# A one-core decoder trunk: first tiles summed earlier, the odd mixer's order changed, and 24 unread products in each round of the local attention

## The chip, the core and the metric

The kernel runs on one core of one Trainium2 chip. The metric is device time in microseconds (us) of one launch, from which a median of several runs is taken. TensorE's granted clock, shown in the profile as a share of full speed, has two levels, 1.2 and 2.4 GHz (0.50 and 1.00).

## What is computed

A two-layer decoder trunk is run over 544 tokens of width 1024: a prompt of 512 tokens and 8 sample streams of 4 tokens each, with the same weights. Each layer is: half a gated feed-forward, a mixer, an attention to 256 memory rows, and half a gated feed-forward again. The first (even) layer mixes with gated linear attention and retention; the second (odd) layer mixes with a diagonal state space (S5) beside a sliding-window attention. Cut to what matters here:

```python
def run_trunk(x, ...):
    for layer in range(2):
        x = x + 0.5 * swiglu(rms_norm(x, w['ffn1_norm'][layer]), gate, up, down)
        h = rms_norm(x, w['mix_norm'][layer])
        x = x + (gla_retention_mixer if layer % 2 == 0 else s5_swa_mixer)(h, ...)
        x = x + memory_attend(rms_norm(x, w['mem_x_norm'][layer]), ...)
        x = x + 0.5 * swiglu(rms_norm(x, w['ffn2_norm'][layer]), gate, up, down)

def s5_swa_mixer(h, ...):
    u, q, k, v = split_cols(h @ odd_w_in)
    c_out = s5_scan(u, ...)          # y = C h + D u; z = gelu(y); z * sigmoid(z @ w_glu + b)
    q, k = partial_rotary(rms_norm(q), pos), partial_rotary(rms_norm(k), pos)
    d_out = sliding_window_sink_attention(q, k, v, ...)   # window 128, 8 heads, 2 key heads
    return concatenate([c_out, d_out]) @ odd_w_out
```

## The kernel before, in words

Tokens lie along the free dimension, features on the 128 partitions; a matrix product turns 128 rows of weights and 272 tokens at a time. Every fp32 weight and activation is split in a high and a low part, and each product is three passes: high by high, high by low, low by high.

**Dense layers.** `projection` (line 105) does all of them but the mixers' and the memory's. It makes output tiles in pairs, s = 0 and 1; a tile of the feed-forward's first half has 8 steps k of 6 products (3 passes, 2 halves of the tokens), 48 in all. SP loads the weights of tile s into `raw[s]`, ACT makes the high part (line 87), DVE the low part (line 91), and TensorE runs the products (line 404). DVE then takes the tile out of PSUM: `finish_tile`, which multiplies by the RMS factor `rstd` (line 295) and, in a feed-forward, joins gate and up tile, or adds to x (line 311). With `norm` the projection also finds `rstd` itself: squares are summed by a product with ones (`sums`, line 396), then ACT takes Ln and Exp (lines 258, 261). With `prepared` the sum of squares of x and 7 of 8 source tiles are already there from the section before, so that only the last step k waits for anything. In the kernel before, the sum stands in the middle of the second tile. The projections that are both `norm` and `prepared` are three: the first halves of ffn2 in layer 0, ffn1 in layer 1 and ffn2 in layer 1. The feed-forward ffn1 of layer 0 has `norm` alone. ACT may overwrite the high weights of tile s only when TensorE has done that tile (`tile_done`).

**The odd mixer** (`odd_mixer`, line 2435) is one section in which each engine has its list of steps written out by hand. TensorE's steps are `dense(i, g)`, tile i of 14 and token half g (line 2658; tiles 0 to 9 are the input projection, 10 to 13 the gate of S5, with 4 steps k); `outputs(q)` for S5 (taps at line 2712, states at line 2716, then ACT's gelu at line 2917); `sums` and `swap` for the norm and rotation of keys and queries (lines 2727, 2736); and then the attention, which runs in five rounds: four blocks of 128 queries (3, 2, 1, 0) and the samples ("s"). Blocks 3 to 1 see 256 keys, block 0 has 128, the samples have 160. A round has two key heads kv = 0 and 1, and goes through these steps:

- `scores(r)` on TensorE (line 2777; for the samples lines 2769 and 2770, and ahead of all `cached_scores`, line 2754), two rounds ahead;
- `soft(r, kv)` on DVE: scale and mask (line 3165), maximum (3168), its negative (3170). It waits for the sink's column, which POOL writes (line 2635);
- `exps(r, kv)` on ACT (line 2951);
- `divide(r, kv)` on DVE (lines 3176 and 3178);
- `turn(r, kv)` on TensorE, the transposes of the probabilities (line 2795), and `turned_copy` on ACT (line 2965);
- `values(r)` on TensorE (line 2819; samples 2811 and 2813), and `out_copy` on ACT (lines 2976, 2973).

Besides, ACT takes four sigmoids of S5's gate (`gates`, line 2983), and POOL multiplies them in (line 2639), in the list of the kernel before behind round 0 on ACT and behind round 1's sinks on POOL. A section ends at a barrier of all engines; the next one, the output projection, splits the mixer's result (lines 264 and 356) and multiplies.

Of the kernel before, what the change touches and what calls it, by code (L numbers as in the profile page):

```python
# [104 lines left out]
def projection(nc, core, name, weights, pairs, kt, src, cols, finish, dst, scale=1.0, after=None, norm=None, scaled=False,  # L105
# [27 lines left out]
    with ExitStack() as ctx:  # L133
# [39 lines left out]
        with nc.Block(name) as block:  # L173
# [112 lines left out]
            def _(dve):  # L286
# [75 lines left out]
                def pair_parts(i):  # L362
                    for s in range(2):
                        split_low(s, i * 2 + (s + 2))
                        finish_tile(s, i)
                        next_part(i, s)
                times_range(dve, 0, last_pair, pre, pair_parts)
                if after is not None:
                    split_low(0, 2 * pairs, after[1])
                finish_tile(0, last_pair)  # L370
# [4 lines left out]
            def _(pe):  # L375
                def tile(s, i, first=False):
                    if not (first and s == 0):
                        pe.wait_ge(low_ready, i * 2 + s)
                    if not first:

                        if finish == "gate":
                            pe.wait_ge((gate_scaled, up_scaled)[s], i)
                        else:
                            pe.wait_ge(psum_free[s], i)
                    for k in range(kt):
                        if norm and first and s == 0 and prepared:
                            if k == kt - 1:
                                pe.wait_ge(last_ready, 1)
                        elif norm and first and s == 0:
                            pe.wait_ge(x_ready, k + 1)  # L390
                        if split and first and s == 0:
                            pe.wait_ge(part_ready, k + 1)
                        if norm and first and s == 1 and k == kt // 2:
                            pe.wait_ge(added, 1 if prepared else 7)
                            for a in range(groups):
                                ins = nc.tensor.matmul(sums[:, a, :], core.mats[:, ONES],
                                                       total[:, a * width:(a + 1) * width], start=True, stop=True)
                            ins.then_inc(summed, 1)
# [9 lines left out]
                for s in range(2):  # L408
                    tile(s, 0, True)
                def pair_tiles(i):  # L410
                    for s in range(2):
                        tile(s, i)
# [2022 lines left out]
def odd_mixer(nc, core, a, out, after_in):  # L2435
# [23 lines left out]
    rounds = [3, 2, 1, "s", 0]  # L2459
    NR = len(rounds)  # L2460

    with ExitStack() as ctx:
# [101 lines left out]
        with nc.Block("odd") as block:  # L2564
# [27 lines left out]
            def _(pool):  # L2592
# [32 lines left out]
                for r in range(NR):  # L2625
# [17 lines left out]
            def _(pe):  # L2643
# [58 lines left out]
                def outputs(q):  # L2702
# [6 lines left out]
                    for t in range(L):  # L2709
                        b, lo = 6 + t // 2, (t % 2) * NCH  # L2710
                        for s in range(t + 1):
                            nc.tensor.matmul(ps[:, b, lo:lo + NCH], taps[:, q, t - s, :], u_tiles[q][:, s:TOK:L],
                                             start=(s == 0), stop=False)
                        for ri in range(2):
                            for j4 in range(4):
# [818 lines left out]
```

## Time and profile before

| | us |
|---|---|
| median of 3 runs (lowest to highest) | 2762.49 (2759.56 to 2765.79) |
| the profiled execution | 2762.19 |
| its span, first to last instruction | 2760.4 |
| TensorE busy (matmuls) | 2562.1 |
| DVE, ACT, POOL busy | 1253.2, 928.2, 452.7 |
| mean granted TensorE clock | 0.96 |

The profiled execution lies 0.3 us below the median; 1.8 us of it lie around the span. TensorE has work for 93% of the span, so time is lost only where it waits and where its clock is at the lower level. The 40 slices of the page show which stretches those are: both mixers' ends, the two memory attentions, and starts of sections.

### The profile page before, as it was taken

To read this page: it belongs to the slowest core of one execution; us is meant where nothing else is said; L and a number is where in the kernel's file an instruction comes from. 1 tells how busy PE (TensorE), PEld (TensorE's weight loads), DVE (VectorE), ACT (ScalarE), POOL (GpSimd) and SP (SyncE) were. 2 spreads that over 40 slices of the span, in tenths; PEclk is the share of its full clock that TensorE was granted. 3 is DMA by queue.
4 is the path that set the end of the run, shared out by engine and by line. 5 is a ranking of instruction groups with operands and counts; after the bars stand their busy time and mean duration, and the time that the engine had idled before them with its cause. 6 is when DMAs were issued, how large, how long until landed. Compare 5 with 4: busy or idle time off the path is not lost. (4 is left out here: it accounts for less than half of the span.)

```text
span 2760.4 us, 48499 instructions
## 1 busy us (share of the span) xinstructions
PE 2562.1 (93%) x20495; PEld 2468.6 (89%) x20495; DVE 1253.2 (45%) x1606; ACT 928.2 (34%) x1128; POOL 452.7 (16%) x464
## 2 busy tenths in 40 slices
PE   6999999998988799999999999999888879999998
PEld 6999998997987699999999999997768859999998
DVE  4433435344555444334434345454655753442442
ACT  4421223222364344212234324231545532431221
POOL 0000012012412220000151464030114223000000
PEclk9999999998999899999999999999989989999999
DMA  3222223211255222222222222221114542222222
GB/s 108 90 92 77 88 88 101 100 49 57 98 178 202 96 77 84 89 79 91 90 82 91 89 76 86 89 68 50 48 47 153 191 145 77 84 88 78 85 95 75
DMA packets 79006, 257.39 MB, mean 93 GB/s; under 512 B 16100, under 2 KB 18740, under 8 KB 78368
## 3 DMA queue, kind: packets, MB, share of 16 engines
q1 hardware_dynamic: 66048, 212.89, 24.2%
q0 software_dynamic: 12832, 42.66, 4.6%
q8 instruction: 98, 1.61, 0.2%
q14 instruction: 28, 0.23, 0.0%
HBM read 245.41 MB, written 10.11 MB: 93 GB/s over the span
## 5 line engine op out<-in xcount | busy, mean ns | idle before, releaser
L91 DVE TENSOR_TENSOR w_low<-w_raw,w_high 128x1024 fp32r<-128x1024 f32 (+1 forms) x358 | 481.7, 1346 | 1031.9 <-ACT w_high L87 1031.6
L87 ACT ACTIVATE w_high<-w_raw 128x1024 fp32r<-128x1024 f32 (+1 forms) x358 | 397.5, 1111 | 1192.4 <-PE ps L404 941.9
L404 PE MATMUL ps<-ffn_hid,w_high 128*128 128x272 f32 x2816 | 476.5, 292 | 24.6 <-PEq L173 24.6
L404 PE MATMUL ps<-h_high,w_high 128*128 128x272 f32 x1920 | 404.1, 292 | 46.2 <-DVE h_low L338 15.6
L404 PEld LDWEIGHTS ps<-ffn_hid,w_high 128*128 128x128 f32 x2816 | 406.1, 192 | 26.1 <-issue 26.1
L404 PE MATMUL ps<-h_high,w_low 128*128 128x272 f32 x1920 | 401.4, 291 | 0.0
L404 PE MATMUL ps<-h_low,w_high 128*128 128x272 f32 x1920 | 401.0, 291 | 0.0
L404 PEld LDWEIGHTS ps<-h_high,w_high 128*128 128x128 f32 x1920 | 306.9, 191 | 49.9 <-DVE h_low L356 16.9
L404 PEld LDWEIGHTS ps<-h_low,w_high 128*128 128x128 f32 x1920 | 307.1, 192 | 0.0
L404 PEld LDWEIGHTS ps<-h_high,w_low 128*128 128x128 f32 x1920 | 304.6, 192 | 0.0
L404 PE MATMUL ps<-ffn_high,w_high 128*128 128x272 f32 x1408 | 292.5, 289 | 12.6 <-DVE ffn_up_sg L295 8.3
L404 PE MATMUL ps<-ffn_hid,w_low 128*128 128x272 f32 x1408 | 295.6, 292 | 0.0
L404 PE MATMUL ps<-ffn_low,w_high 128*128 128x272 f32 x1408 | 292.8, 289 | 0.0
L404 PE MATMUL ps<-ffn_high,w_low 128*128 128x272 f32 x1408 | 291.7, 289 | 0.0
L404 PEld LDWEIGHTS ps<-ffn_high,w_high 128*128 128x128 f32 x1408 | 222.2, 189 | 13.9 <-DVE w_low L91 8.7
L404 PEld LDWEIGHTS ps<-ffn_hid,w_low 128*128 128x128 f32 x1408 | 225.4, 192 | 0.0
L404 PEld LDWEIGHTS ps<-ffn_high,w_low 128*128 128x128 f32 x1408 | 222.3, 189 | 0.0
L404 PEld LDWEIGHTS ps<-ffn_low,w_high 128*128 128x128 f32 x1408 | 221.6, 189 | 0.0
L203 POOL TENSOR_TENSOR rstd<-x 128x544 f32<-128x544 f32 x7 | 7.6, 1090 | 897.8 <-DVE x L311 897.8
L627 PE MATMUL ps<-h_high,w_high 128*128 128x272 f32 (+1 forms) x400 | 123.8, 310 | 1.7 <-PEq L67 1.7
L627 PE MATMUL ps<-h_high,w_low 128*128 128x272 f32 (+1 forms) x400 | 119.5, 299 | 0.0
L627 PE MATMUL ps<-h_low,w_high 128*128 128x272 f32 (+1 forms) x400 | 119.3, 298 | 0.0
(497 smaller groups left out, 3619.9 us busy)
## 6 DMA issues: line engine op xcount, KB each, us to landing
w_raw<-in_ffn_w_gate SPq DMA_DIRECT2D x88, 512.0 KB, 3.6
w_raw<-in_ffn_w_up SPq DMA_DIRECT2D x88, 512.0 KB, 3.6
w_raw<-in_ffn_w_down SPq DMA_DIRECT2D x64, 704.0 KB, 4.1
mem_ring<-in_cache_mem_k POOLq DMA_DIRECT2D x64, 256.0 KB, 6.3
mem_ring<-in_cache_mem_v POOLq DMA_DIRECT2D x64, 256.0 KB, 6.3
w_raw<-in_even_w_in SPq DMA_DIRECT2D x24, 512.0 KB, 3.6
w_raw<-in_mem_w_q SPq DMA_DIRECT2D x16, 512.0 KB, 4.9
w_raw<-in_mem_w_k SPq DMA_DIRECT2D x16, 512.0 KB, 4.4
```

What stands on the lines that cost most here:

```text
L87: return nc.scalar.activation(core.high[s][:, 0:kt * P], core.raw[s][:, 0:kt * P], ACT.Copy)
L91: return nc.vector.tensor_tensor(core.low[s][:, 0:kt * P], core.raw[s][:, 0:kt * P], core.high[s][:, 0:kt * P].bitcast(F32), ALU.subtract)
L203: nc.gpsimd.tensor_tensor(rstd, x, x, ALU.mult).then_inc(squares_added, 1)
L404: last = nc.tensor.matmul(acc[s][:, a, :], w, x[:, k, a * width:(a + 1) * width], start=(k == 0 and n == 0), stop=(k == kt - 1 and n == 2))
L627: ins = nc.tensor.matmul(ps[0:m, g, 0:HALF], w[:, k * width:k * width + m], x[:, k, g * HALF:(g + 1) * HALF], start=(k == 0 and p == 0), s ...
```

## The change

In `projection`: the prepared first pair runs steps 0 to 6 of tile 0, then the sum of squares, then steps 0 to 6 of tile 1, and only then step 7 of both tiles. And DVE takes a finished tile out of PSUM before it makes the next low weights, where it was the other way round. In `odd_mixer`: the samples' round comes second; the gate's sigmoids come behind the exponentials of the round before the last, and POOL's four products behind all sinks; norm and rotation of the last query tiles come ahead of the gate's low parts on DVE; the scores of round 0 and of the cache come ahead of tile 11 on TensorE, with the softmax steps moved to match; the taps of S5's outputs are joined, two time steps in one product; and 24 products of 272 columns into an unused bank (8 ahead of each turn and 8 ahead of the values) are added in each round.

```diff
@@ projection, DVE @@
                     for s in range(2):
+                        finish_tile(s, i)
                         split_low(s, i * 2 + (s + 2))
-                        finish_tile(s, i)
                         next_part(i, s)
@@ projection, TensorE @@
+                def sum_squares():
+                    pe.wait_ge(added, 1 if prepared else 7)
...
+                def first_pair():
+                    if norm and prepared:
+
+                        products(0, range(kt - 1))
+                        sum_squares()
+                        pe.wait_ge(low_ready, 1)
+                        products(1, range(kt - 1))
+                        pe.wait_ge(last_ready, 1)
+                        for s in range(2):
+                            products(s, [kt - 1]).then_inc(tile_done, 1)
+                        return
@@ odd_mixer @@
-    rounds = [3, 2, 1, "s", 0]
+    rounds = [3, "s", 2, 1, 0]
@@ odd_mixer, POOL @@
-                    if r == 1:
-                        for t in range(4):
-                            pool.wait_ge(sig_ready, t + 1)
-                            nc.gpsimd.tensor_tensor(u_tiles[t], u_tiles[t], sig[:, t], ALU.mult).then_inc(gated, 1)
+                for t in range(4):
+                    pool.wait_ge(sig_ready, t + 1)
+                    nc.gpsimd.tensor_tensor(u_tiles[t], u_tiles[t], sig[:, t], ALU.mult).then_inc(gated, 1)
@@ odd_mixer, TensorE, outputs(q) @@
-                    for t in range(L):
-                        b, lo = 6 + t // 2, (t % 2) * NCH
-                        for s in range(t + 1):
-                            nc.tensor.matmul(ps[:, b, lo:lo + NCH], taps[:, q, t - s, :], u_tiles[q][:, s:TOK:L],
-                                             start=(s == 0), stop=False)
...
+                    u = u_tiles[q].rearrange("p (c s) -> p s c", s=L)
+                    for h in range(2):
+                        for d in range(2 * h + 2):
+                            t = max(2 * h, d)
+                            lo = (t - 2 * h) * NCH
+                            nc.tensor.matmul(ps[:, 6 + h, lo:2 * NCH], taps[:, q, d, :], u[:, t - d:2 * h + 2 - d, :],
+                                             start=(d == 0), stop=False)
...
@@ odd_mixer, TensorE @@
+                def keep_busy(r):
+
+                    if r == 0:
+                        pe.wait_ge(evicted, 2 * NT)
+                    for _ in range(8):
+                        nc.tensor.matmul(ps[:, 0, 0:HALF], core.h[0][:, 0, 0:P], core.h[0][:, 1, 0:HALF], start=True, stop=True)
...
                 turn_values()
+                swap(4)
                 dense(10, 0)
                 dense(10, 1)
-                swap(4)
+                scores(0)
+                cached_scores()
                 dense(11, 0)
                 dense(11, 1)
-                scores(0)
-                cached_scores()
...
                 for r in range(NR):
+                    keep_busy(r)
                     turn(r, 0)
+                    keep_busy(r)
                     turn(r, 1)
                     if r + 2 < NR:
                         scores(r + 2)
+                    keep_busy(r)
                     values(r)
@@ odd_mixer, ACT @@
-                    if r == 0:
+                    if r == NR - 2:
                         gates()
@@ odd_mixer, DVE @@
+                norm(4)
+                rotate(3)
                 z_low_part(0)
                 z_low_part(1)
-                norm(4)
+                rotate(4)
                 z_low_part(2)
                 z_low_part(3)
-                rotate(3)
+                pick_samples()
...
```

What it does to the instruction lists is shown at three places.

POOL, in the attention: line 2635 writes the sinks' columns, line 2639 multiplies by the gates. Before:

```order
L2635 TENSOR_SCALAR odd_region<-vectors 128x4 x4
L2639 TENSOR_TENSOR odd_mixed<-odd_mixed,s_gd 128x544 x4
L2635 TENSOR_SCALAR odd_region<-vectors 128x4 x2
L2635 TENSOR_SCALAR odd_region<-vectors 128x1 x2
L2635 TENSOR_SCALAR odd_region<-vectors 128x4 x2
```

and now (lines 2653 and 2656):

```order
L2653 TENSOR_SCALAR odd_region<-vectors 128x4 x2
L2653 TENSOR_SCALAR odd_region<-vectors 128x1 x2
L2653 TENSOR_SCALAR odd_region<-vectors 128x4 x6
L2656 TENSOR_TENSOR odd_mixed<-odd_mixed,s_gd 128x544 x4
```

The four gate products no longer stand ahead of any sink.

ACT, from the exponentials of the round before the last to the end, now: lines 2984 exponentials, 2998 copies of the turned probabilities, 3016 sigmoids, 3009 copies of results.

```order
L3009 ACTIVATE odd_mixed<-ps 128x4x128
L2998 ACTIVATE odd_region<-ps 128x1024
L2984 ACTIVATE odd_region,s_rot<-odd_region,s_rot 128x129 x4
L2998 ACTIVATE odd_region<-ps 128x1024
L2984 ACTIVATE odd_region,s_rot<-odd_region,s_rot 128x129 x4
L3016 ACT_TABLE_LOAD
L3016 ACTIVATE s_gd<-s_gd 128x544 x4
L3009 ACTIVATE odd_mixed<-ps 128x4x128
L2998 ACTIVATE odd_region<-ps 128x512 x2
L3009 ACTIVATE odd_mixed<-ps 128x4x128
```

The table load and the sigmoids stand behind the last exponentials and ahead of the copies of the last two results; the second table load of the list before, back to the exponentials, is gone.

TensorE, the first round of the attention, now: 2851 the added products, 2818 turns, 2800 scores, 2842 values.

```order
L2851 MATMUL ps<-h_high 128x272 x8
L2818 MATMUL ps<-mats,odd_region 128x128 x8
L2851 MATMUL ps<-h_high 128x272 x8
L2818 MATMUL ps<-mats,odd_region 128x128 x8
L2800 MATMUL ps<-odd_k,odd_mixed 128x256 x8
L2851 MATMUL ps<-h_high 128x272 x8
L2842 MATMUL ps<-odd_region,s_rot 64x512 x4
```

Between any two steps of a round that wait for another engine there are now 8 products that wait for none.

## Rows read from the trace of the kernel before

**Rows 1.** The page: busy time, share of the span and instructions of TensorE.
```profile
PE 2562.1 (93%) x20495; PEld 2468.6 (89%) x20495; DVE 1253.2 (45%) x1606; ACT 928.2 (34%) x1128; POOL 452.7 (16%) x464
```

**Rows 2.** Waits of TensorE, whole span: us in total, times, longest us.
```profile
PE ps L404 <- DVE ffn_up_sg L295: 16.1, 4, 4.3
PE ps L2795 <- DVE odd_region L3178: 12.2, 3, 7.9
```

**Rows 3.** Stretches: us, busy PE, PEld, DVE, ACT, POOL, clock, DMA share, GB/s.
```profile
1989.00:1996.00 7.00, 6.18 (x26) 4.41 (x28) 4.59 (x6) 5.69 (x17) 0.00 (x0) 0.51 0.00 0
1996.00:2003.00 7.00, 2.59 (x16) 1.14 (x12) 0.63 (x1) 5.09 (x8) 5.78 (x7) 0.98 0.00 0
2003.00:2013.00 10.00, 6.55 (x22) 3.73 (x22) 9.32 (x16) 5.07 (x17) 0.21 (x1) 0.50 0.00 0
2024.00:2040.00 16.00, 11.36 (x55) 8.50 (x55) 5.24 (x8) 7.79 (x18) 0.00 (x0) 0.50 0.11 33
2040.00:2050.00 10.00, 10.00 (x81) 10.00 (x81) 4.83 (x7) 1.81 (x2) 1.09 (x1) 0.99 0.33 107
```

**Rows 4.** Timeline, attention: start us, us, instruction [idle before <-releaser].
```profile
1984.60 1.23 DVE L3178 TENSOR_TENSOR odd_region<-odd_region,s_rot 128x1024 f32<-128x1024 f32 x1
...
1994.83 1.28 ACT L2983 ACT_TABLE_LOAD   x1
1996.12 2.30 ACT L2983 ACTIVATE s_gd<-s_gd 128x544 f32<-128x544 f32 x4
...
1996.86 5.22 POOL L2639 TENSOR_TENSOR odd_mixed<-odd_mixed,s_gd 128x544 f32<-128x544 f32 x4 [24.53 <-ACT s_gd L2983]
...
2002.37 1.23 DVE L3165 SCALAR_TENSOR_TENSOR odd_region<-ps,w_raw 128x1024 f32<-128x1024 f32 x1 [8.68 <-POOL odd_region L2635]
...
2032.77 0.60 ACT L2976 ACTIVATE odd_mixed<-ps 128x512 f32<-128x512 f32 x1 [2.07 <-PE ps L2819]
```

**Rows 5.** Timeline, TensorE at full clock: scores, a turn, values.
```profile
1982.36 2.00 PE L2777 MATMUL ps<-odd_k,odd_mixed 64*128 64x256 f32 x16
1985.88 1.09 PE L2795 MATMUL ps<-mats,odd_region 128*128 128x128 f32 x8 [1.53 <-DVE odd_region L3178]
...
2017.83 1.94 PE L2819 MATMUL ps<-odd_region,s_rot 128*64 128x512 f32 x8
```

**Rows 6.** Timeline, first pair of ffn2's first half, layer 0.
```profile
1000.64 1.08 PE L396 MATMUL ps<-rstd,mats 128*128 128x272 f32 x4
1001.75 0.72 ACT L258 ACTIVATE rstd<-ps,eps 128x544 f32<-128x544 f32 x1 [7.29 <-PE ps L396]
...
1005.75 1.06 ACT L87 ACTIVATE w_high<-w_raw 128x1024 fp32r<-128x1024 f32 x1
1006.84 1.23 DVE L91 TENSOR_TENSOR w_low<-w_raw,w_high 128x1024 fp32r<-128x1024 f32 x1 [11.39 <-ACT w_high L87]
1007.98 0.72 DVE L295 TENSOR_TENSOR ffn_up_sg<-ps,rstd 128x544 f32<-128x544 f32 x1
...
1008.85 0.49 PE L404 MATMUL ps<-ffn_high,w_high 128*128 128x272 f32 x2 [4.15 <-DVE ffn_up_sg L295]
```

**Rows 7.** Stretches behind TensorE's waits (columns as in rows 3), and one wait.
```profile
1009.00:1013.00 4.00, 4.00 (x21) 4.00 (x21) 2.58 (x3) 2.33 (x3) 0.00 (x0) 0.57 0.62 151
743.00:747.00 4.00, 4.00 (x34) 4.00 (x33) 3.15 (x2) 1.01 (x2) 2.14 (x2) 1.00 0.92 316
...
742.34 0.49 PE L1627 MATMUL ps<-even_next_high,w_high 128*128 128x272 f32 x2 [1.49 <-PEq L67]
```

**Rows 8.** Timeline, the gate's tiles: low part, norm, rotation on DVE; TensorE's wait.
```profile
1962.87 0.77 DVE L3130 SCALAR_TENSOR_TENSOR odd_mixed<-odd_mixed,vectors,s_scratch 128x544 f32<-128x544 f32 x1
...
1969.60 0.72 DVE L3140 TENSOR_TENSOR s_scratch<-ps,odd_sin 128x544 f32<-128x544 f32 x1 [0.45 <-PE ps L2736]
...
1963.01 0.40 PE L2658 MATMUL ps<-h_high,w_high 128*128 128x272 f32 x1 [1.09 <-DVE h_low L3124]
```

**Rows 9.** Timeline, S5 outputs and a sum: strided taps, states, unstrided 272 columns.
```profile
1885.80 2.18 PE L2712 MATMUL ps<-odd_mixed,odd_region 128*128 128x136 f32 x8
1887.91 0.67 PE L2716 MATMUL ps<-odd_hs,s_ct 128*32 128x136 f32 x16
...
1955.63 1.08 PE L2727 MATMUL ps<-s_scratch,mats 128*128 128x272 f32 x4
```

More of the change, by code:

```diff
@@ L375, in _, with products @@
             def _(pe):
[L376 to L398, printed above, removed]
+                def products(s, ks):
+                    for k in ks:
                         w_high = core.high[s][:, k * P:(k + 1) * P]
@@ L405, in tile, with whole @@
                                                         start=(k == 0 and n == 0), stop=(k == kt - 1 and n == 2))
-                    last.then_inc(tile_done, 1)
-                for s in range(2):
-                    tile(s, 0, True)
+                    return last
+                def whole(s):
+                    products(s, range(kt)).then_inc(tile_done, 1)
+                def sum_squares():
+                    pe.wait_ge(added, 1 if prepared else 7)
+                    for a in range(groups):
+                        ins = nc.tensor.matmul(sums[:, a, :], core.mats[:, ONES], total[:, a * width:(a + 1) * width],
+                                               start=True, stop=True)
+                    ins.then_inc(summed, 1)
+                def first_pair():
[8 more added lines that the diff above has]
+                        return
+                    for k in range(kt):
+                        if norm:
+                            pe.wait_ge(x_ready, k + 1)
+                        if split:
+                            pe.wait_ge(part_ready, k + 1)
+                        last = products(0, [k])
+                    last.then_inc(tile_done, 1)
+                    pe.wait_ge(low_ready, 1)
+                    products(1, range(kt // 2))
+                    if norm:
+                        sum_squares()
+                    products(1, range(kt // 2, kt)).then_inc(tile_done, 1)
                 def pair_tiles(i):
                     for s in range(2):
-                        tile(s, i)
+                        pe.wait_ge(low_ready, i * 2 + s)
+                        if finish == "gate":
+                            pe.wait_ge((gate_scaled, up_scaled)[s], i)
+                        else:
+                            pe.wait_ge(psum_free[s], i)
+                        whole(s)
+                first_pair()
                 times_range(pe, 1, pairs, pre, pair_tiles)
@@ L2708, in outputs @@
                         pe.wait_ge(z_ready, q)
-                    for t in range(L):
-                        b, lo = 6 + t // 2, (t % 2) * NCH
-                        for s in range(t + 1):
-                            nc.tensor.matmul(ps[:, b, lo:lo + NCH], taps[:, q, t - s, :], u_tiles[q][:, s:TOK:L],
-                                             start=(s == 0), stop=False)
-                        for ri in range(2):
-                            for j4 in range(4):
-                                ins = nc.tensor.matmul(ps[32 * j4:32 * j4 + 32, b, lo:lo + NCH], ct[:, ri, t, 4 * q + j4, :],
-                                                       hs[:, q % 2, ri, j4, :], start=False, stop=(ri == 1))
+                    u = u_tiles[q].rearrange("p (c s) -> p s c", s=L)
[5 more added lines that the diff above has]
+                                             start=(d == 0), stop=False)
+                        for t in (2 * h, 2 * h + 1):
+                            lo = (t - 2 * h) * NCH
+                            for ri in range(2):
+                                for j4 in range(4):
+                                    ins = nc.tensor.matmul(ps[32 * j4:32 * j4 + 32, 6 + h, lo:lo + NCH],
+                                                           ct[:, ri, t, 4 * q + j4, :], hs[:, q % 2, ri, j4, :],
+                                                           start=False, stop=(ri == 1 and t == 2 * h + 1))
                     ins.then_inc(used, 1)
@@ L3042, in _ @@
                 w_high(12)
+                exps(0, 0)
                 w_high(13)
-                exps(0, 0)
+                exps(0, 1)
                 w_high(14)
-                exps(0, 1)
                 for r in range(NR):
```

10 lines of the change are left out of this document (4 added, 6 removed).

## The prediction

> **What bounds the kernel now.** I read the page first: TensorE has work for 93% of the span [rows 1], so only its waits and its slow clock can be won, and every moved step counts by what it does to TensorE's list. Then the waits of TensorE over the whole span. Two of them lie where the diff works: it waits four times, 16.1 us in all, for the first tile of a feed-forward to be scaled, and 12.2 us for the divided probabilities of the attention [rows 2]. One of the four waits stands in the feed-forward that isn't prepared and stays. Then the stretches of the attention, read for the granted clock: 0.51, 0.98, 0.50 and 0.50 of full speed [rows 3]. The first drop follows turns with idle time between them, and the next one 7 us in which TensorE had 2.6 us of work. Last the timelines, which say who is late.
>
> **First tiles of the three prepared projections.** The chain before, from layer 0's ffn2 [rows 6]: TensorE sums the squares at 1000.6 in the middle of tile 1, ACT takes Ln at 1001.75, Exp and its table follow, then the high part of the next weights at 1005.75 (1.06 us), DVE's low part (1.23) and only then the scaling (0.72). TensorE, whose second tile ends at 1004.7 (1008.85 less the 4.15 it waited), goes on at 1008.85. Now the sum comes after 42 of 96 products, some 3.8 us earlier (30 products at 0.125), so ACT has rstd ready at about 1000.6, before either tile ends. What is late next: both tiles end together. Tile 0 is done only 0.75 us (6 products) before tile 1, at 1003.95, and ACT may not overwrite its weights sooner. From there 1.06 for the high part, 1.23 for the low part and 0.15 of signals make 1006.4, while the scaling now runs beside ACT. TensorE waits 1.7 us instead of 4.15: 2.45 won.
>
> The wait has a second price. After it TensorE ran at a mean clock of 0.57 for 4 us [rows 7], so 1.7 us were lost; the other two places show the same. After a wait of 1.49 the clock stayed at 1.00 [rows 7]. The new wait of 1.7 lies nearer to that one, so I take the clock's loss as gone: 2.45 + 1.7 = 4.15 each, 12.5 for three. Bounds: 7.3 if the clock falls all the same, 12.9 if the wait too is gone.
>
> The other order on DVE (evict first, low weights second) I cost at nothing: both are due a whole tile later, 48 products or 6 us, and together take under 5 us. Without that cover, each tile would show 0.7 us. SP's loads, which follow the low weights, leave up to 3 us later and have some 4 us of slack.
>
> **S5's outputs.** Ten tap products of 136 columns become six of 272 or 136 with the same columns in all. One pass over 136 strided columns takes 0.27 us (2.18 for 8), one over 272 columns side by side takes 0.27 as well (1.08 for 4), and 136 unstrided ones, four running at once, 0.17 (0.67 for 16) [rows 9]. If the 0.27 is a price per pass, four products of two passes go in each of four blocks: 8.6 us won. If it is the price of the stride, nearly nothing is. The unstrided 0.17 is below 0.27, so the stride is charged, and I take 0.3 won; bounds 0 and 8.6. The Trainium skill (SBUF — State Buffer, Door 1: The DMA port swizzle) says that SBUF has lines of 16 bytes and that each access to a new line pays a penalty; four fp32 values are one line, and here each column is the fourth value. By that rule the term is about 0 and not 8.6.
>
> **The gate's tiles.** DVE now makes the norm and two rotations ahead of the last two low parts of tile 10. A norm is 0.77 and a rotation 1.44 (two operations of 0.72); the norm stood ahead of these two before [rows 8]. So TensorE, which already waited 1.09 there, gets step 2 of tile 10 some 2.9 us later. The swap that stood between tiles 10 and 11 now runs in that wait: 0.8 back. Scores and cache products only change places with tile 11. At the end tile 13 waits 1.3 us, since its low part stands behind the second softmax; in return that softmax no longer lies between tile 13 and the first division, about 0.9 back. Sum: 2.5 lost, between 0 and 4.5.
>
> **The local attention.** Before, it lasts from the first division at 1984.6 to the last copy's end at 2033.4: 48.8 us [rows 4]. Its largest stall is a queue: ACT loads the sigmoid's table (1.28) and takes four sigmoids (2.30), POOL multiplies for 5.22 behind them, the sinks of the next round stand behind POOL's products, and DVE waits 8.68 for them [rows 4]. That stall goes. What is late next is TensorE itself. At full clock a full turn takes 1.0, scores of 256 keys 1.83, values 1.87 (each row's length less its overlap with the next step) [rows 5]. The list: six full turns 6.0, two of samples and two of block 0 1.7; scores 1.83 + 1.83 + 1.1; values 3 x 1.87, 2.6 for the samples, 0.95 for block 0; 21.6 in all, where the small ones are estimates by size. To it come the products. TensorE's rate at full clock is 81 in 10 us [rows 3], so eight take 1.0; one group runs before the first division is done, 14 groups make 14.0. They were meant for idle time, but with the stall gone little is left: a group runs while ACT copies a turn (free), the other two a round mostly delay the values and the next turn. Now the waits: 1.3 for the first division, about 1.0 in small ones, and 1.85 in the last round, since the sigmoids (3.6 us) now stand on ACT ahead of the copy that the last values need. With 0.6 for the last copy that is 21.6 + 14.0 + 4.15 + 0.6 = 40.4. So 8.4 won, if the clock stays up. Without the products the same chain gives 36 us at full clock and 42 at a mean of 0.7; before, the clock was low for some 33 of these 49 us. So they cost about what they bring. POOL's gate products, now last, end about 1 us before the last copy and are hidden.
>
> **The output projection** started at half clock until 2040 [rows 3]. It could start warm, but the barrier's gap of some 3 us stands, so I take 0.2 won, bounds 1.9 won and nothing.
>
> **Sum.** 12.5 + 0.3 - 2.5 + 8.4 + 0.2 = 18.9 won against the profiled execution: 2762.2 - 18.9 = 2743.3. That execution lies 0.3 below the median of 2762.49, so 2743.5.
>
> **The rivals.** (a) The clock still falls after the 1.7 us waits: 3 x 1.7 = 5.1 less is won, 2748.5. For it: no row here has a wait between 1.5 and 4 us that kept the clock; against it, the wait of 1.49 is the nearer one. (b) The joined taps run at a price per pass: 8.3 more is won, 2735. Against it the 0.17. (c) The products hold the clock only in part and win nothing in the attention. 35.6 us of TensorE's list at clock c and 4.75 of waits give 48.8 at c = 0.81; then 2752. (d) Slower: the products, in the attention's rounds on TensorE, turn from filler into load. At half clock the list takes 71.2 and the stage some 76: 27 us more than before, and with the 10.5 won elsewhere 2779. It decides from c = 0.65 downward, where the stage reaches 59.3 us and eats all the other gains. Against it speaks that TensorE would then have work without a break, and in the unbroken work of the output projection the clock is at 0.99 from 2040 on [rows 3]; for it, that turns and values kept it at 0.50 for 16 us. (e) The change doesn't do what it says: the stall moves, from POOL's queue to the sigmoids on ACT at the end, and the first tiles wait for the weights as long as for rstd. Then only 0.5 won and 2.5 lost remain: 2764, within 0.2%.
>
> **How the numbers follow.** 0.2% is 5.5 us, about what a measurement of this kernel can tell from no change. Chances: the forecast 0.58, (a) 0.17, (b) 0.09, (c) 0.08, (d) 0.04, (e) 0.04. All but (d) and (e) are faster by over 0.2%: 0.92, and 0.04 each for same and slower. The time is that of the forecast. The range runs from 2736, near (b) or the taps' partial gain with the gate's tiles at no loss, to 2754, which takes in (a) with the gate's tiles at their worst and (c).
>
> **What would show it.** Right: TensorE's wait for the scaled first tile gone, and one of 1.5 to 2 us for the low weights in its place at three points, with the clock at 1.00 behind it; no wait of DVE for POOL's sink columns; the attention about 40 us from first division to last copy with a clock above 0.95 and TensorE hardly idle but before the last turn; taps at 0.5 us a pass over 272 columns; the first division some 2.5 us later after the last tile of the input projection. Wrong: a low clock in the attention (c, d), taps at 0.27 a pass (b), a drop behind the first tiles (a).

## The result and the profile after

The changed kernel took 2743.05 us (median of 4 runs, 2741.61 to 2749.17) against 2761.96 for the kernel before beside it (4 runs): a ratio of 0.9934, 95% interval 0.9916 to 0.9953, so faster, by 18.9 us. The profiled execution took 2742.95 with a span of 2741.2; before, that span was 2760.4. The forecast was 2743.5.

The page's busy line answers to [rows 1] (VectorE is DVE there, ScalarE is ACT, GpSimd is POOL). TensorE is busy for as long as before: the 120 added products and its faster clock about cancel. VectorE has the same 1606 instructions, but 74 us more of busy time. That comes with its new order in the projection: x4 below, which has the old order, is back at 1252.7.

```profile
PE 2562.7 (93%) x20583; PEld 2468.6 (90%) x20583; DVE 1327.3 (48%) x1606; ACT 917.3 (33%) x1127; POOL 479.6 (17%) x464
```

**First tiles.** The list of TensorE's waits (us in total, times, longest) has no line for the scaled first tile any more [rows 2]; this one stands there. Its seven waits for the weights' low part are the three prepared first tiles (1.67, 1.66 and 1.67), the unprepared one (2.31) and three new ones, of which more below.

```profile
PE ps L383 <- DVE w_low L91: 10.6, 7, 2.3
```

The timeline of layer 0's ffn2, to be read beside [rows 6]: the sum of squares comes first, rstd is ready at 997.55 (996.89 and 0.66 of Exp), well before the tiles end; both ACT's high part and VectorE's scaling start as the first tile ends, and TensorE goes on after 1.67.

```profile
993.75 1.08 PE L393 MATMUL ps<-rstd,mats 128*128 128x272 f32 x4
...
1000.91 1.06 ACT L87 ACTIVATE w_high<-w_raw 128x1024 fp32r<-128x1024 f32 x1 [2.06 <-PE ps L383]
...
1000.91 0.72 DVE L295 TENSOR_TENSOR ffn_up_sg<-ps,rstd 128x544 f32<-128x544 f32 x1 [8.53 <-PE ps L383]
1002.00 1.22 DVE L91 TENSOR_TENSOR w_low<-w_raw,w_high 128x1024 fp32r<-128x1024 f32 x1 [0.37 <-ACT w_high L87]
...
1003.28 0.52 PE L383 MATMUL ps<-ffn_high,w_high 128*128 128x272 f32 x2 [1.67 <-DVE w_low L91]
```

The stretches (columns as in [rows 3]) behind this wait in the unprepared first feed-forward and in the three prepared ones, then the attention, then two behind the 3.18 us wait for the output projection. The granted clock is the third figure from the right.

```profile
38.00:42.00 4.00, 3.89 (x31) 3.89 (x32) 3.54 (x6) 1.77 (x4) 0.00 (x0) 1.00 0.48 131
1003.00:1007.00 4.00, 3.72 (x29) 3.72 (x30) 3.54 (x6) 1.88 (x3) 0.00 (x0) 1.00 0.48 135
1415.00:1419.00 4.00, 4.00 (x32) 4.00 (x33) 3.54 (x5) 1.95 (x3) 3.50 (x7) 1.00 0.36 131
2338.00:2342.00 4.00, 4.00 (x33) 4.00 (x33) 3.42 (x5) 1.83 (x3) 0.00 (x0) 1.00 0.36 131
1979.00:2021.00 42.00, 37.92 (x288) 29.07 (x286) 25.03 (x43) 25.83 (x77) 7.39 (x10) 1.00 0.05 15
2024.00:2026.00 2.00, 2.00 (x11) 2.00 (x10) 1.50 (x4) 2.00 (x4) 0.00 (x0) 0.50 0.42 170
2026.00:2028.00 2.00, 2.00 (x13) 2.00 (x13) 2.00 (x3) 1.40 (x3) 0.00 (x0) 0.65 0.00 0
```

**Attention.** The timeline, against [rows 4]. The first division starts at 1979.02, the last copy ends at 2020.90: 41.9 us against 48.8. No wait of VectorE for a sink column is left. Eight products take 1.28 and keep the next step off for 1.09 to 1.21 (1.12 from 1988.59 to 1989.71); ACT's sigmoids stand ahead of the copy that the last turn needs, and that is TensorE's longest wait, 1.62.

```profile
1979.02 1.22 DVE L3211 TENSOR_TENSOR odd_region<-odd_region,s_rot 128x1024 f32<-128x1024 f32 x1
...
1980.30 1.09 PE L2818 MATMUL ps<-mats,odd_region 128*128 128x128 f32 x8 [0.82 <-DVE odd_region L3211]
...
1988.59 1.28 PE L2851 MATMUL ps<-h_high 128*128 128x272 f32 x8
1989.71 0.27 PE L2813 MATMUL ps<-mats,odd_region 128*128 128x128 f32 x1
...
2012.91 1.28 ACT L3016 ACT_TABLE_LOAD   x1
2014.20 2.30 ACT L3016 ACTIVATE s_gd<-s_gd 128x544 f32<-128x544 f32 x4
...
2017.61 0.63 PE L2818 MATMUL ps<-mats,odd_region 128*128 128x128 f32 x4 [1.62 <-ACT odd_region L2998]
...
2023.43 0.52 PE L383 MATMUL ps<-h_high,w_high 128*128 128x272 f32 x2 [3.18 <-DVE h_low L356]
...
2020.30 0.60 ACT L3009 ACTIVATE odd_mixed<-ps 128x512 f32<-128x512 f32 x1 [1.43 <-PE ps L2842]
```

**A new loss.** A feed-forward runs as two half sections, each with gate and up tiles and then, behind a wait of 3.08, the products that lead down. In the second half section of layer 1's first feed-forward TensorE waits three times where it didn't wait before. VectorE's operations behind the tile that ends at 1620.1 show why: from the scaling to the end of the low part they take 7.0 us, with the last one 2.07 in place of 1.22 in the timeline above.

```profile
1620.13 0.72 DVE L295 TENSOR_TENSOR ffn_up_up<-ps,rstd 128x544 f32<-128x544 f32 x1 [3.03 <-PE ps L383]
1620.89 1.33 DVE L301 TENSOR_TENSOR ffn_up_prod<-ffn_up_sg,ffn_up_up 128x544 f32<-128x544 f32 x1
1622.37 1.06 DVE L305 TENSOR_SCALAR ffn_hid<-ffn_up_prod 128x544 f32 x1
1623.56 1.60 DVE L307 TENSOR_TENSOR ffn_hid<-ffn_up_prod,ffn_hid 128x544 f32 x1
1625.08 2.07 DVE L91 TENSOR_TENSOR w_low<-w_raw,w_high 128x1024 fp32r<-128x1024 f32 x1
...
1627.20 0.52 PE L383 MATMUL ps<-h_high,w_high 128*128 128x272 f32 x2 [1.09 <-DVE w_low L91]
...
1652.73 0.52 PE L383 MATMUL ps<-h_high,w_high 128*128 128x272 f32 x2 [1.11 <-DVE w_low L91]
...
1666.12 0.52 PE L383 MATMUL ps<-h_high,w_high 128*128 128x272 f32 x2 [1.11 <-DVE w_low L91]
```

**Where the 19.2 us of span went**, from the starts of TensorE's work behind the same waits in both traces (a negative figure is won):

| stretch | before | after | difference |
|---|---|---|---|
| up to layer 0's ffn2 (the unprepared first tile is in it) | 991.49 | 988.41 | -3.08 |
| ffn2 of layer 0, both halves | 416.77 | 411.74 | -5.03 |
| ffn1 of layer 1, first half | 211.77 | 207.67 | -4.10 |
| ffn1 of layer 1, second half | 205.86 | 210.02 | +4.16 |
| S5 (to the first sum of the rotations) | 103.90 | 103.83 | -0.07 |
| from there to the attention's first turn | 56.09 | 58.63 | +2.54 |
| first turn to output projection | 50.03 | 43.13 | -6.90 |
| output projection | 51.78 | 51.39 | -0.39 |
| memory, layer 1 | 248.21 | 248.15 | -0.06 |
| ffn2 of layer 1, both halves | 424.50 | 418.23 | -6.27 |

### The profile page after: what moved, and what is told of

It reads as the page before. It is cut to its first block and busy times, and to the rows that moved or that the text cites. A ratio compares the mean times of both kernels' runs of the same rounds, so it can differ in the third digit from the quotient of the medians.

```text
span 2741.2 us, 48674 instructions
## 1 busy us (share of the span) xinstructions
PE 2562.7 (93%) x20583; PEld 2468.6 (90%) x20583; DVE 1327.3 (48%) x1606; ACT 917.3 (33%) x1127; POOL 479.6 (17%) x464
## 5 line engine op out<-in xcount | busy, mean ns | idle before, releaser
L91 DVE TENSOR_TENSOR w_low<-w_raw,w_high 128x1024 fp32r<-128x1024 f32 (+1 forms) x358 | 505.0, 1411 | 186.0 <-ACT w_high L87 185.7
L311 DVE SCALAR_TENSOR_TENSOR x<-ps,x 128x544 f32<-128x544 f32 (+1 forms) x96 | 69.6, 725 | 365.4 <-PE ps L383 365.4
L295 DVE TENSOR_TENSOR ffn_up_up<-ps,rstd 128x544 f32<-128x544 f32 x88 | 63.7, 724 | 304.0 <-PE ps L383 304.0
L295 DVE TENSOR_TENSOR ffn_up_sg<-ps,rstd 128x544 f32<-128x544 f32 x88 | 63.7, 724 | 193.3 <-PE ps L383 188.6
```

Source lines behind the costliest of these rows:

```text
L91: return nc.vector.tensor_tensor(core.low[s][:, 0:kt * P], core.raw[s][:, 0:kt * P], core.high[s][:, 0:kt * P].bitcast(F32), ALU.subtract)
L295: nc.vector.tensor_tensor(in_groups(to[:], cols), acc[s], in_groups(rstd, cols), ALU.mult).then_inc((gate_scaled, up_scaled)[s], 1)
L311: ins = nc.vector.scalar_tensor_tensor(out, acc[s], scale, out, ALU.mult, ALU.add)
```

## The experiments

### The parts of the change

In x1 the products are left out, nothing else.

```diff
-                    keep_busy(r)
                     turn(r, 0)
-                    keep_busy(r)
                     turn(r, 1)
...
-                    keep_busy(r)
                     values(r)
```

> The changed kernel without the 24 products a round. Main theory (they cost about what they bring): the granted clock falls in the attention; from the first division to the last copy it takes 40 to 44 us instead of 41.9, and the whole 2741 to 2746 us. Rival 1 (they are load only, the clock stays up without them): 36 to 37 us, the whole about 2738. Rival 2 (they carry the gain): 46 us or more, the whole over 2747.

Measured: 2746.27, ratio 0.9956 (0.9941 to 0.9970). From the first division to the last copy it took 41.7 against 41.9 with the products, and from the first turn to the output projection 42.92 against 43.13. TensorE was busy for 31 of 41 us at a mean clock of 0.75, against 37.9 of 42 at 1.00 above:

```profile
1975.00:2016.00 41.00, 30.72 (x172) 18.44 (x172) 23.79 (x43) 25.91 (x77) 7.25 (x10) 0.75 0.05 13
```

So the products held the clock, as meant, and cost what it brought.

x2 has the changed projection with the old odd mixer, x3 the changed odd mixer with the old projection. Of the many lines in which x2 differs from the changed kernel, one stands for all:

```diff
...
-    rounds = [3, "s", 2, 1, 0]
+    rounds = [3, 2, 1, "s", 0]
...
```

> The kernel before with the new first pair and DVE order in the projection alone. Main theory (the projection carries most of the gain): 12 to 14 us less than before, about 2749, with the waits of 1.67 us in the three prepared first pairs, a clock of 1.00 behind them, and the three new waits of 1.1 us in the second half of layer 1's ffn1, which cost about 4 us. Rival (much of it was the chance of where the clock fell): 7 to 9 us less, 2754.

> The kernel before with the odd mixer's part of the change alone. Main theory (stage by stage: 2.5 lost ahead of the attention, 6.9 won in it, 0.4 behind): 4 to 6 us less than before, about 2757. Rival (the attention wins more once its start is not shifted by the earlier part): 8 us less or more.

Measured: x2 2752.49, ratio 0.9972 (0.9962 to 0.9982); x3 2754.23, 0.9980 (0.9968 to 0.9991). x2 is 7.4 us below the kernel before that was run beside it (2759.86): the rival's number, and not the 12 to 14 of the main theory. The trace shows what that theory named all the same. The projection alone has the waits of 1.67, 1.66 and 1.67, but also the three new ones, and the attention at 50.03 as before:

```profile
1624.85 0.52 PE L383 MATMUL ps<-h_high,w_high 128*128 128x272 f32 x2 [1.09 <-DVE w_low L91]
...
1997.21 1.97 PE L2813 MATMUL ps<-mats,odd_region 128*128 128x128 f32 x8 [7.86 <-DVE odd_region L3196]
```

The odd mixer alone, 5.6 us below, as its main theory had it, has the old first-tile waits (4.15, 4.27, 4.15), 205.88 in the half section that got slower, and 44.59 in the attention, where three other traces with this mixer took 43.13 to 43.15. The difference is the clock. In x3 it fell in the middle of TensorE's unbroken work, behind the values of the samples:

```profile
2007.00:2011.00 4.00, 4.00 (x26) 3.97 (x25) 3.69 (x4) 0.47 (x4) 0.00 (x0) 0.60 0.00 0
```

So the products don't hold the clock every time, and why it fell there isn't settled. The two gains, 0.28% and 0.20%, make 0.48% of the whole's 0.66%, at the lower edge of its interval (0.47 to 0.84).

### VectorE's order and its neighbour

x4 is the changed kernel with the low weights ahead of the eviction, as before.

```diff
                     for s in range(2):
-                        finish_tile(s, i)
                         split_low(s, i * 2 + (s + 2))
+                        finish_tile(s, i)
...
```

> The changed kernel with DVE's old order in the projection (low weights first, then the tile). Main theory (the new order makes the new waits in layer 1's ffn1, since DVE and POOL slow each other there, and shortens the first tiles' waits elsewhere): the waits of 1.1 us in that half go, 4 us won; the first pair of layer 0's ffn1 waits 3.6 us again with a low clock behind, 2.6 lost; the three prepared first pairs wait 2.4 instead of 1.67, 0.7 lost each or 2.4 if the clock falls. The whole 2743 to 2749. Rival (the order is worth nothing, and the new waits have another cause): they stay, and the whole is within 1 us of the changed kernel.

Measured: 2742.83, ratio 0.9945 (0.9928 to 0.9961). The three waits are gone and that half section takes 205.87. In return the three first tiles wait 2.4 each instead of 1.67, and the unprepared one goes on at 39.31 instead of 38.11 (after a wait of 2.42, where 3.6 was expected). The total came within a us of the changed kernel's, as the rival had it, but its reason is wrong, since the waits went. The order by itself gives with one hand what it takes with the other.

But why do these waits stand in this half section alone? GpSimd makes S5's tables beside it. x10 keeps the changed order and cuts two of every three operations of that table work, the second product and the sum, to one column, so the tables, and the results that follow from them, are not the reference's.

```diff
+            if d > 0:
+                part, to = part[:, 0:1, 0:1, 0:1], to[:, 0:1, 0:1, 0:1]
...
-                step(g.tensor_tensor(part, c[:, 1 - ri], ai, ALU.mult))
-                step(g.tensor_tensor(to, to, part, op))
+                step(g.tensor_tensor(part[:, 0:1, 0:1], part[:, 0:1, 0:1], part[:, 0:1, 0:1], ALU.mult))
+                step(g.tensor_tensor(to[:, 0:1, 0:1], to[:, 0:1, 0:1], part[:, 0:1, 0:1], op))
```

> The changed kernel, in which GpSimd's table work beside the second half of layer 1's first feed-forward leaves out the second product and the sum of each complex power (one column in place of 512), so the tables and the result that follow from them are not the reference's. Main theory (the three new waits of some 1.1 us there come from VectorE's operations, stretched while GpSimd works beside them): the low part behind the first gate product takes 1.2 to 1.5 us in place of 2.07, at most one of the waits is left, and that half section takes 206 to 208 us against 210.0. Rival (the order of VectorE's list alone makes them): the three waits stay and the half section takes 209.5 to 210.5.

Measured: 2734.55 (2 runs), ratio 0.9909 (0.9886 to 0.9933). All three waits are gone, the half section takes 205.86, and the same five operations of VectorE take 4.7 us (1622.89 to 1627.6) instead of 7.0:

```profile
1622.89 0.72 DVE L295 TENSOR_TENSOR ffn_up_up<-ps,rstd 128x544 f32<-128x544 f32 x1 [3.70 <-PE ps L383]
1623.65 0.73 DVE L301 TENSOR_TENSOR ffn_up_prod<-ffn_up_sg,ffn_up_up 128x544 f32<-128x544 f32 x1
1624.52 1.09 DVE L305 TENSOR_SCALAR ffn_hid<-ffn_up_prod 128x544 f32 x1
1625.73 0.73 DVE L307 TENSOR_TENSOR ffn_hid<-ffn_up_prod,ffn_hid 128x544 f32 x1
1626.38 1.22 DVE L91 TENSOR_TENSOR w_low<-w_raw,w_high 128x1024 fp32r<-128x1024 f32 x1
```

That shows the cause: it takes both, the new order (x4, without it, has no such wait) and GpSimd's work beside it. The scaling, which reads PSUM beside one SBUF operand, takes 0.72 in either; the three operations with two SBUF inputs stretch (0.73 to 1.33 and 1.60, 1.22 to 2.07). In the changed kernel each of them ends 0.6 to 1.1 us after the GpSimd operation that had started before it; for the last one (it ends at 1627.15) that is this operation, which ends at 1626.06:

```profile
1624.65 1.41 POOL L2375 TENSOR_TENSOR s_gd<-s_gd,s_prm 128x512 f32<-128x512 f32 x1
```

The Trainium skill (SBUF — State Buffer, SBUF: two separate sides) says that VectorE and GpSimd share a pair of ports that one of them holds for a whole instruction, and that an operation of VectorE with two SBUF inputs needs it against a GpSimd operation that reads SBUF. The three operations agree with that. L305, which has one SBUF input, stretches too: it takes 1.06 here and 1.09 in x10, and 0.44 in the quiet first pair of layer 0. The two inputs alone therefore don't say which operations are stretched, and no run here separates that.

### The attention's parts

x5 is the kernel before with one move, GpSimd's gate products behind all sinks. x6 is the kernel before with the products alone.

```diff
-                    if r == 1:
-                        for t in range(4):
+                for t in range(4):
```

> The kernel before with one edit: GpSimd multiplies the gates only after it has written the sinks of all rounds; the sigmoids stay behind round 0 on ScalarE, and no products are added. Main theory (the 8.68 us stall of VectorE behind GpSimd's gate product, not the missing products, is what cost the local attention its time): no VectorE wait on GpSimd over 1 us is left, and the stretch from the first turn to the output projection, 50.0 before, takes 42 to 45. Rival (the stall only moves, to the sigmoids on ScalarE or to the next sum): that stretch takes 47 or more. The rest of the program within 2 us of the kernel before, apart from the first tiles' clock.

```diff
...
+                    keep_busy(r)
                     turn(r, 0)
+                    keep_busy(r)
                     turn(r, 1)
...
+                    keep_busy(r)
                     values(r)
```

> The kernel before with one edit: the 24 products a round. Main theory: the stall behind GpSimd's gate product stays (over 6 us of waiting on VectorE in the second round), the clock still falls in it, and the stretch from the first turn to the output projection takes 48 to 52 against 50.0. Rival (the products by themselves hold the clock, and that is the gain): 45 or less. Rival (the products load a TensorE at half clock): over 53.

Measured: x5 2753.38, ratio 0.9974 (0.9963 to 0.9986); x6 2763.65, 1.0010 (0.9997 to 1.0023). In x5 VectorE's wait for a sink column is gone. In x6 it is still there (8.4), with TensorE's stall behind it, and behind that the clock falls (a row of the timeline, then the stretch):

```profile
2004.80 1.97 PE L2795 MATMUL ps<-mats,odd_region 128*128 128x128 f32 x8 [7.05 <-DVE odd_region L3188]
```

```profile
2004.00:2012.00 8.00, 7.20 (x28) 5.37 (x30) 7.36 (x14) 4.51 (x16) 0.21 (x1) 0.53 0.01 2
```

| kernel | first turn | output projection | between |
|---|---|---|---|
| before | 1985.88 | 2035.91 | 50.03 |
| x6, products only | 1984.52 | 2037.97 | 53.45 |
| x5, gate products last only | 1982.39 | 2026.68 | 44.29 |
| x1, changed without products | 1975.07 | 2017.99 | 42.92 |
| changed | 1980.30 | 2023.43 | 43.13 |
| x7, below: 8 products a round | 1973.01 | 2014.87 | 41.86 |
| x8, below: none | 1976.26 | 2019.81 | 43.55 |

One moved step makes 5.7 of the 6.9 won. The products alone make the stage 3.4 longer, outside what the main theory allowed and by its number the last rival's case: where they delay work and a stall takes the clock all the same, they are load. The stage is read from one trace; the total of x6 lies 4.8 above the kernel before that was run beside it, and the interval of the ratio still holds 1.

### A version that keeps the gains

x7 takes from the experiments: evict first in the first pair alone, the last tiles of the odd mixer's projection in the old order, the sigmoids back behind round 0, and products only ahead of the second turn, where TensorE waits for ACT's copy. x8 is x7 without products.

```diff
-                times_range(dve, 0, last_pair, pre, pair_parts)
+                pair_parts(0, True)
+                times_range(dve, 1, last_pair, pre, pair_parts)
...
-                    keep_busy(r)
                     turn(r, 0)
                     keep_busy(r)
                     turn(r, 1)
...
-                    keep_busy(r)
                     values(r)
...
-                    if r == NR - 2:
+                    if r == 0:
                         gates()
```

> The changed kernel with four edits: VectorE evicts ahead of the weights' low part in the first pair alone and goes back to the old order behind it; the last tiles of the odd mixer's projection in the order of the kernel before; the sigmoids behind round 0, where they were, with GpSimd's gate products behind all sinks; products only ahead of the second turn (8 a round in place of 24). Main theory, against the changed kernel: 4.1 us less in the second half of layer 1's first feed-forward, 2.5 less ahead of the attention, 1.5 to 3 less in it: some 2734, span 2733 (2729 to 2738), first-tile waits of 1.67 as in the changed kernel. Rival (the third of the products does not hold the clock): the attention takes 44 or more from the first turn to the output projection, total 2738 to 2741. Rival (the old order behind the first pair brings the first wait back): 4 us more in each of three stages, 2745.

> As the run before it (first pair alone evicts first, old order of the last tiles, sigmoids behind round 0, GpSimd's gate products last) with no products at all. Main theory (products cost about what they give back): within 2 us of the run before it, the granted clock of the attention below 1.00 in several stretches. Rival (8 products ahead of the second turn lie in a wait for ScalarE's copy and hold the clock for nothing): this one is 2 to 5 us slower than the run before it.

Measured: x7 2731.72 (5 runs), ratio 0.9893 (0.9878 to 0.9907), below both kernels; x8 2737.74, 0.9909 (0.9895 to 0.9924). Against the changed kernel x7 wins 4.33 in the half section (205.69), 3.5 ahead of the attention (55.13; 2.5 were expected), and 1.27 in it (1.5 to 3 were expected).

Of the 4.33 only 2.8 are the order's. x7 still has one of the three waits, 1.11 behind the first pair, and up to the wait of 3.08 it takes 136.99, against 139.81 in the changed kernel and 135.60 in x4. The rest is the clock behind that wait: 1.00 in x7, 0.64 in the changed kernel (1748 to 1752), and 0.50 in x8, which has the order of x7 and takes 208.42 for the half section. First x7, then x8:

```profile
1744.50:1748.50 4.00, 4.00 (x33) 4.00 (x34) 1.62 (x1) 1.21 (x1) 0.00 (x0) 1.00 0.69 200
```

```profile
1747.50:1751.50 4.00, 4.00 (x18) 4.00 (x19) 1.63 (x1) 1.34 (x1) 0.00 (x0) 0.50 0.58 182
```

x8 lies 6.0 above x7, more than either theory had. But the intervals of the two overlap, and of their difference in span, 8.2 us, only 1.7 lie in the attention. Another 3.25 had come about before the first turn, where the two kernels do the same (1973.01 and 1976.26). Of the difference, then, no more than the 1.7 is shown to be the products' work. In the stage itself x7 runs at a mean clock of 0.87 and x8 at 0.80:

```profile
1973.00:2013.00 40.00, 31.99 (x212) 22.28 (x212) 26.35 (x42) 27.31 (x78) 8.30 (x10) 0.87 0.02 6
```

```profile
1976.00:2018.00 42.00, 29.71 (x172) 17.88 (x172) 26.10 (x43) 27.56 (x78) 8.49 (x10) 0.80 0.02 5
```

x9 is x7 with three products of constants in the wait ahead of the output projection. The same lines also put them ahead of the even mixer's output projection in layer 0.

```diff
+                    if split:
+                        ones = core.mats[:, 0:2, :].rearrange("p m c -> p (m c)")
+                        for _ in range(3):
+                            nc.tensor.matmul(acc[1][:, 0, 0:2 * P], core.mats[:, ONES], ones, start=True, stop=True)
```

> The candidate (first pair alone evicts first, old order of the last tiles, sigmoids behind round 0, 8 products a round) with three products of constants that nobody reads ahead of the output projection, in the last half of its 3.18 us wait for VectorE. Theory (a TensorE that multiplies in the wait keeps its clock): the 2.7 us at half clock that follow the wait are gone, 1.0 to 1.4 us less in the output projection, total some 2730.5. Rival (the 1.7 us that stay idle ahead of them are enough to lose the clock): the half clock stays, no change or up to 0.3 us more.

Measured: 2735.57, ratio 0.9916 (0.9898 to 0.9934), span 2730.3 against 2729.9: no gain that can be told, where some 2730.5 was expected. The clock is held at 1.00, though 1.74 us stay idle ahead of the three; but TensorE, now faster, catches up with VectorE and waits for it 4.9 us later, so the output projection takes 51.01 instead of 51.38, a third of the 1.0 to 1.4 that the theory promised. In layer 0 the three products ran at half clock and outlasted the wait: TensorE went on 0.9 later than after the 11.79 of x7. So the total tests both places at once. First the timeline (a product of this type leaves two records), then two stretches behind the later place:

```profile
687.68 2.90 PE L415 MATMUL ps<-mats 128*128 128x256 f32 x6 [10.33 <-PEq L67]
...
2010.39 1.53 PE L415 MATMUL ps<-mats 128*128 128x256 f32 x6 [1.74 <-PEq L67]
...
2016.74 0.52 PE L387 MATMUL ps<-h_high,w_high 128*128 128x272 f32 x2 [0.76 <-DVE h_low L356]
```

```profile
2013.00:2015.00 2.00, 2.00 (x18) 1.94 (x17) 1.49 (x4) 2.00 (x4) 0.00 (x0) 1.00 0.13 53
...
2017.00:2021.00 4.00, 4.00 (x34) 4.00 (x34) 2.21 (x4) 1.62 (x2) 0.89 (x1) 1.00 0.47 131
```

## Why the prediction was right, and where it was not

The total came out within half a us. That closeness is luck: two steps that failed partly offset each other, the attention won less than was forecast, and the clock elsewhere gave the rest. Executions of kernels that do the same work up to the attention reach its first turn 5.2 us apart (x1 at 1975.07, the changed kernel at 1980.30). What is not luck is the mechanism of the two large terms.

- **The three prepared first tiles (12.5).** This was right in both parts. The waits fell by 2.48, 2.60 and 2.46 (7.5; forecast 7.35). From the first pair to the next wait of the section the stretches shortened by 0.96, 1.50 and 2.55 (5.0; forecast 5.1), with the clock at 1.00 behind each. Rival (a) falls, and not by luck: in all seven traces with the new first pair and VectorE's new order in it the clock behind these waits of 1.66 or 1.67 is 1.00, 21 times of 21.
- **"One of the four waits stands in the feed-forward that isn't prepared and stays".** This failed. There too the scaling now stands ahead of the low weights: TensorE goes on at 38.11 instead of 39.22, and the clock behind it is 1.00 where it was 0.63 (39 to 43 us before). In this execution that is some 2.6 us won that the sum lacked. About half of it is chance. Behind this wait the clock also fell with the new order, to 0.58 to 0.67 in x1, x2, x7 and x10; and the wait of 3.08 that comes next ends at 161.72 to 163.94 in the seven traces with the new order, at 163.38 to 164.42 in the five with the old, 1.3 apart in the mean.
- **"The other order on DVE ... I cost at nothing: both are due a whole tile later ... and together take under 5 us".** This failed in one half section, for 4.16. The durations came from rows where GpSimd was idle; beside its table work the chain takes 7.0 us, more than the tile of 6 that was to hide it. x4 and x10 show it.
- **S5's outputs (0.3).** The stride is charged, as the text had it, so rival (b) falls; but fewer and longer runs win more than 0.3. From the first tap of a block to the last state it takes 7.29 us (1873.39 to 1880.68) against 7.95 (1880.56 to 1888.51 before): 0.38 off the taps, 0.28 off the states, 2.6 in four blocks.

```profile
1873.39 1.69 PE L2732 MATMUL ps<-odd_mixed,odd_region 128*128 128x272 f32 x4 [1.60 <-ACT odd_hs L2945]
1875.00 1.14 PE L2738 MATMUL ps<-odd_hs,s_ct 128*32 128x136 f32 x32
1876.07 3.61 PE L2732 MATMUL ps<-odd_mixed,odd_region 128*128 128x272 f32 x8
1879.61 1.14 PE L2738 MATMUL ps<-odd_hs,s_ct 128*32 128x136 f32 x32
1880.68 4.13 PE L2715 MATMUL ps<-odd_mixed,odd_region 32*128 32x136 f32 x64
```

  In the profiled execution two stretches at about half clock in this stage (0.57 and 0.55 over 3 us each) took it back, hence the -0.07; in x10, with none before its last two us, the stage takes 101.32, 2.6 below before. Joined taps gave 101.3 to 104.9 over eight traces, 103.2 in the mean, the old ones 103.9 in all four. Behind the second of the two waits of 1.60 in this stage the clock of the next 4 us is 0.60 to 0.70 in seven of the eight, and 1.00 in all four with the old taps. Why it falls more often with the joined ones isn't settled.
- **The gate's tiles (+2.5).** This was right: 2.54, with 1.19 for tile 13 where 1.3 was forecast. x7 and x8, in the old order, take it off again.
- **The attention (8.4).** The mechanism was right: the stall is gone, TensorE itself is late, the clock stays at 1.00, and the last round waits 1.62 for the sigmoids (1.85). The mis-sized term is "eight take 1.0": nine groups keep the next step off for 1.09 to 1.21, and the five that a wait follows run for 1.24 to 1.26, so the 14 make 16.6 instead of 14.0. The stage lacks 1.5 of these 2.6 (41.9 instead of 40.4); smaller terms are off the other way. That the products cost about what they bring is borne out by x1. The figures given for that, 36 and 42 us without the products, don't follow from the terms of the sum as it is given; x1 took 41.7 at a mean clock of 0.75. And the 33 us of low clock before are counted on to 2040, past the stage's end at 2033.4: within it the rows have some 26.
- **The output projection (0.2).** It won 0.39, within its bounds; its half clock stayed, 0.50 and 0.65 in the rows above.
- **Rivals (c), (d), (e).** (c) and (d) fall by the clock of 1.00 in the attention, (e) by its 41.9 us and the waits of 1.67. Still, x3 shows that (c) can happen for a few us, and x6 shows that (d) had its place, at a smaller price: without the moved gate products, the products would have cost 3.4 us of that stage.

What the table shows beyond these terms (-3.4 in all, the larger pieces -1.5 behind the 3.08 us wait of the first half section of layer 0's ffn2 and -1.1 in layer 1's last half section) lies behind waits that the change doesn't touch; the last section tells of them.

## What to carry to other kernels

Before an operation is moved behind another on VectorE because the next tile is to hide both, look at what GpSimd does beside it in every stage that runs this code, and take the durations from the worst of them. A stall that ends in a queue is cured by the one move in that queue; try that alone before filler work is added, because filler in a list that has no idle time left cost here what the clock gave (43.13 against 42.92). Where filler is used, put it in a wait that stays, and see who is late next.

## What the runs showed of the hardware

The clock behind a wait of one length isn't always the same. In x4 four waits of 2.39 to 2.42 for the first tile were followed by clocks of 0.60, 1.00, 0.66 and 1.00:

```profile
39.50:43.50 4.00, 4.00 (x21) 4.00 (x22) 2.59 (x3) 2.59 (x3) 0.00 (x0) 0.60 0.45 147
1006.00:1010.00 4.00, 4.00 (x33) 4.00 (x34) 2.58 (x3) 2.26 (x3) 0.00 (x0) 1.00 0.57 147
```

Behind the 3.08 us waits of the feed-forwards it was 1.00 in one place of the changed kernel (1128 to 1132) and 0.57 in another (1539 to 1543). One and the same place gives both, too: behind the wait in the second half section of layer 1's ffn1 the stretch to S5 took 68.70 in x7, at 1.00, and 71.45 in x8, at 0.50, with the same instructions. Such a place is worth up to 2.7 us, and there are eight of them, so spans of kernels that do the same work can differ by several us: x7 and x8, the same up to the attention, reach its first turn at 1973.01 and 1976.26. The time of a stage, not the span, is what a change of a few us should be judged by, and the clock behind each wait in that stage is to be read beside it.
